# Low parts of forty expert tiles made early, kept in DRAM and loaded again

## The reference

```
qb = (xb @ w_q).reshape(TOKEN_BLOCK, PEER_HEADS, 2, PEER_DKEY)
s = jnp.einsum('thcd,hcnd->thcn', qb, sub_keys)
s_top, i_top = lax.top_k(s, PEER_TOPK)
...
best, pos = lax.top_k(cand, PEER_TOPK)
eidx = jnp.take_along_axis(cand_idx, pos, axis=-1)
g = jax.nn.softmax(best, axis=-1)
h = jax.nn.gelu(jnp.einsum('td,thkd->thk', xb, u[eidx]), approximate=False)
out = jnp.einsum('thk,thkd->td', g * h, v[eidx])
```

## Time and profile before

| | us |
|---|---|
| median of 3 runs | 1611.57 (1611.14 to 1612.08) |
| profiled execution | 1614.49 |
| its span in the profile | 1612.7 |
| TensorE busy (PE) | 1577.1 (98%) |
| VectorE busy (DVE) | 1281.4 (79%) |
| ScalarE busy (ACT) | 630.0 (39%) |
| GpSimd busy (POOL) | 517.4 (32%) |
| data moved | 427.05 MB |

### The profile page before, as it was taken

How to read it: one execution, slowest core, us unless ns; L and a number is a source line. 1 busy time by engine, 2 the same in 40 slices (tenths; PEclk the granted TensorE clock), 3 DMA queues, 4 the chain that set the end, 5 groups by cost and what they waited for, 6 DMA issues and landing times.

```text
span 1612.7 us, 24488 instructions
## 1 busy us (share of the span) xinstructions
PE 1577.1 (98%) x9566; PEld 1389.2 (86%) x9566; DVE 1281.4 (79%) x2390; ACT 630.0 (39%) x996; POOL 517.4 (32%) x261
## 2 busy tenths in 40 slices
PE   9999999999999999899999989999999999999998
PEld 7897977888989999889999988888888888888886
DVE  3024366246899999999998789999999999999997
ACT  5324445523223333345455333333333434333332
POOL 4433232361235778421010233333332232222200
PEclk9999999999999999999999999999999999999999
DMA  5342112133124669699998999999999999999972
GB/s 203 142 149 84 58 53 79 60 135 147 53 92 138 186 199 303 214 331 315 350 354 256 291 420 398 392 396 394 387 391 422 413 409 415 392 391 410 399 297 78
DMA packets 141633, 427.05 MB, mean 265 GB/s; under 512 B 11344, under 2 KB 73040, under 8 KB 120272
## 3 DMA queue, kind: packets, MB, share of 16 engines
q1 hardware_dynamic: 118224, 274.47, 46.9%
q0 software_dynamic: 23296, 151.04, 23.8%
HBM read 378.77 MB, written 46.14 MB: 263 GB/s over the span
## 4 chain that ended last, share of the span: by engine, by line
PE 62%; DVE 31%; DMA 3%; issue 2%; ACT 1%; POOL 0%; SPq 0%; DVEq 0%
PE bank L1437 19%; PE bank L1439 18%; PE bank L1438 18%; DVE wlo L1265 5%; DVE acc L1311 4%; DVE uvb L1273 4%; PE bank L1743 3%; DMA raw<-in_u 2%; DVE idx L1179 1%; DVE idx L1171 1%; DVE val L1170 1%; DVE val L1178 1%; DVE tmp L1172 1%; DMA raw<-in_uv 1%; DVE uvb L1283 1%
## 5 line engine op out<-in xcount | busy, mean ns | idle before, releaser
L1437 PE MATMUL bank<-xhi,whi 128*128 128x352 f32 (+1 forms) x1408 | 491.2, 349 | 22.8 <-DVE wlo L1265 13.8
L1439 PE MATMUL bank<-xhi,wlo 128*128 128x352 f32 (+1 forms) x1408 | 480.8, 341 | 0.0
L1438 PE MATMUL bank<-xlo,whi 128*128 128x352 f32 (+1 forms) x1408 | 480.7, 341 | 0.0
L714 POOL DMA_INDIRECT uvb<-in_uv,eidx x128 | 200.2, 1564 | 571.9 <-DVE acc L1311 422.3
L896 ACT ACTIVATE whi<-raw 128x1024 fp32r<-128x1024 f32 x255 | 268.7, 1055 | 207.1 <-PE bank L1439 148.8
L1437 PEld LDWEIGHTS bank<-xhi,whi 128*128 128x128 f32 x1408 | 265.2, 188 | 50.6 <-DVE wlo L1265 25.1
L1265 DVE TENSOR_TENSOR wlo<-raw,whi 128x1024 fp32r<-128x1024 f32 x215 | 261.9, 1219 | 44.6 <-ACT whi L896 44.4
L1437 PE MATMUL bank<-whi,ahi 128*128 128x512 f32 x762 | 296.7, 389 | 0.0
L1438 PE MATMUL bank<-wlo,ahi 128*128 128x512 f32 x762 | 296.7, 389 | 0.0
L1439 PE MATMUL bank<-whi,alo 128*128 128x512 f32 x762 | 296.5, 389 | 0.0
L1439 PEld LDWEIGHTS bank<-xhi,wlo 128*128 128x128 f32 x1408 | 265.3, 188 | 15.5
(11 more groups left out here) (225 smaller groups left out, 1860.8 us busy)
## 6 DMA issues: line engine op xcount, KB each, us to landing
raw<-in_u SPq DMA_DIRECT2D x128, 512.0 KB, 6.3
raw<-in_uv SPq DMA_DIRECT2D x127, 512.0 KB, 9.2
g_scratch<-stage SPq DMA_DIRECT2D x48, 512.0 KB, 6.9
gl<-g_scratch SPq DMA_DIRECT2D x32, 768.0 KB, 9.6
raw<-in_w_in SPq DMA_DIRECT2D x22, 1024.0 KB, 4.9
h_scratch<-hout SPq DMA_DIRECT2D x96, 192.0 KB, 5.3
hl<-h_scratch SPq DMA_DIRECT2D x24, 768.0 KB, 11.0
raw<-in_w_q SPq DMA_DIRECT2D x6, 1024.0 KB, 4.7
```

What stands on the lines that cost most here:

```text
L714: nc.gpsimd.indirect_dma_start(out=uvb[:, r % UVB, :], out_offset=None, in_=a["uv"][:, :], in_offset=bass.IndirectOffsetOnAxis(ap=eidx[:, ...
L1437: mm(out, lh, rh, start=first, stop=False)
L1438: mm(out, lh, rl, start=False, stop=False)
L1439: return mm(out, ll, rh, start=False, stop=last)
```

## The change

For the first 40 u tiles (`NPRE`) the low part is made during the projections and attention and put into a DRAM tensor. ScalarE issues the loads and stores and makes a rounded copy, VectorE subtracts. 13 turns (`PRE_PROJ` = 40 - 27) stand behind the evacuations of the last projection tiles before attention, one in each of the 27 slots of attention. Three buffers of 4 KB a partition and one for the copy lie in the place of `xn`, so x is loaded there later, once all stores have landed. In the u stage SP loads such a tile's low part beside the tile itself; GpSimd makes none, and has only its gathers. The step constants move some four to six steps forward, and the pairs of sums are spread anew.

```diff
-FIRST_FUSED = 96
+FIRST_FUSED = 92
-POOL_ONLY = 40
-EXP_STEP = 39
-NORM_STEP = 43
-PICKS_TILE = 42
-PICKS_STEP = 46
-HOT0, HOT1, HOT2 = 48, 86, 90
-C_STEPS = [41, 42, 43, 44, 45, 47] + [49 + 3 * i for i in range(NCP - 6)]
-C_TILE, C_STEP = 80, 80
+NPRE = 40
+DVE_FIRST = 34
+EXP_STEP = 34
+NORM_STEP = 37
+PICKS_TILE = 37
+PICKS_STEP = 41
+HOT0, HOT1, HOT2 = 42, 80, 84
+C_STEPS = [34, 35, 36, 38, 39, 40] + [43 + 3 * i for i in range(NCP - 6)]
+C_TILE, C_STEP = 76, 76
-GL_FIRST, GL_SECOND = 95, 99
+GL_FIRST, GL_SECOND = 90, 94
-SUM_STEPS = [89, 91, 93, 95] + [97 + i * 59 // 29 for i in range(29)] + [156 + i * 94 // 31 for i in range(31)]
+SUM_STEPS = [84, 86, 88, 90] + [92 + i * 68 // 29 for i in range(29)] + [160 + i * 90 // 31 for i in range(31)]
...
+        pre_raw = place("pre_raw", [P, 3, D], F32, xn_at)
+        pre_hi = place("pre_hi", [P, D], F32R, xn_at + 3 * 4 * D)
...
@@ wait_low
-            if s < POOL_ONLY:
-                engine.wait_ge(low_pool, s + 1)
+            if s < NPRE:
+                engine.wait_ge(lo_in[s % 4], 16 * (s // 4 + 1))
...
@@ SP
-            sp.wait_ge(x_split_lo, KD)
-            sp.dma_start(xn[:, :, :], a["x_n"]).then_inc(x_in, 16)
...
+            for i in range(3):
+                sp.wait_ge(pre_out[i], 16 * len(range(i, NPRE, 3)))
+            sp.dma_start(xn[:, :, :], a["x_n"]).then_inc(x_in, 16)
             for g in range(G_WO, G_WQ):
...
@@ SP, tile_load
+                elif s >= NPRE + 4:
+                    wait_low(sp, s - 4)
                 elif s >= 4:
-                    wait_low(sp, s - 4)
+                    sp.wait_ge(tile_hi, s - 3)
...
+                if s < NPRE:
+                    if s >= 4:
+                        sp.wait_ge(h_done, s - 3)
+                    else:
+                        sp.wait_ge(q_done, 14 + 2 * (s // 2))
+                    sp.dma_start(tile_bufs(s)[2].bitcast(F32), lo_dram[s]).then_inc(lo_in[s % 4], 16)
...
@@ GpSimd
-            for s in range(POOL_ONLY):
-                tile_low(s)
...
+            pool.wait_ge(cidx_done, 1)
...
+            for j in range(NCP):
                 gather_u(j)
...
@@ ScalarE
+            def pre_load(i):
+                if i >= 3:
+                    act.wait_ge(pre_out[i % 3], 16 * (i // 3))
+                act.dma_start(pre_raw[:, i % 3, :], a["u"][i]).then_inc(pre_in[i % 3], 16)
+
+            def pre_store(i):
+                act.wait_ge(pre_low, i + 1)
+                act.dma_start(lo_dram[i], pre_raw[:, i % 3, :]).then_inc(pre_out[i % 3], 16)
+
+            def pre_turn(i):
+                if i >= 1:
+                    pre_store(i - 1)
+                if i + 1 < NPRE:
+                    pre_load(i + 1)
+                act.wait_ge(pre_in[i % 3], 16 * (i // 3 + 1))
+                nc.scalar.activation(pre_hi[:, :], pre_raw[:, i % 3, :], ACT.Copy).then_inc(pre_high, 1)
...
             for n in range(2 * N_DIL):
                 proj_evac(n)
+                if n == 3:
+                    act.wait_ge(x_split_lo, KD)
+                    pre_load(0)
+                if n >= 2 * N_DIL - PRE_PROJ:
+                    pre_turn(n - 2 * N_DIL + PRE_PROJ)
...
@@ ScalarE, slot s of attention, after the exponentials and before the squares
+                pre_turn(PRE_PROJ + s)
...
@@ VectorE
+            def low_ahead(i):
+                dve.wait_ge(pre_high, i + 1)
+                r = pre_raw[:, i % 3, :]
+                V.tensor_tensor(r, r, pre_hi[:, :].bitcast(F32), ALU.subtract).then_inc(pre_low, 1)
+
+            for i in range(PRE_PROJ):
+                low_ahead(i)
...
@@ VectorE, at the end of slot s of attention
+                low_ahead(PRE_PROJ + s)
...
-            for s in range(POOL_ONLY, 2 * NT):
-                tile_low(s)
+            for s in range(DVE_FIRST, 2 * NT):
+                if s >= NPRE:
+                    tile_low(s)
```

More of the change, by code:

```diff
@@ L208, in program @@
         xlo = keep("xlo", [P, KD, S], F32R)
+        xn_at = at["top"]
         xn = keep("xn", [P, TC, D])
+        pre_raw = place("pre_raw", [P, 3, D], F32, xn_at)
+        pre_hi = place("pre_hi", [P, D], F32R, xn_at + 3 * 4 * D)
         raw = keep("raw", [P, 2, GC])
@@ L387, in program @@
         g_dram = nc.dram_tensor("g_scratch", [NT // 4, P, SETS, 4, SET], F32, kind="Internal").ap()
+        lo_dram = nc.dram_tensor("lo_scratch", [NPRE, P, D], F32, kind="Internal").ap()
         def sem(name):
@@ L422, in program @@
         traw = [sem(f"traw{i}") for i in range(4)]
-        tile_hi, low_pool, low_dve = sem("tile_hi"), sem("low_pool"), sem("low_dve")
+        tile_hi, low_dve = sem("tile_hi"), sem("low_dve")
+        pre_in = [sem(f"pre_in{i}") for i in range(3)]
+        pre_out = [sem(f"pre_out{i}") for i in range(3)]
+        pre_high, pre_low = sem("pre_high"), sem("pre_low")
+        lo_in = [sem(f"lo_in{i}") for i in range(4)]
         h_done, h_gelu = sem("h_done"), sem("h_gelu")
@@ L438, in wait_low @@
         def wait_low(engine, s):
-            if s < POOL_ONLY:
-                engine.wait_ge(low_pool, s + 1)
+            if s < NPRE:
+                engine.wait_ge(lo_in[s % 4], 16 * (s // 4 + 1))
             else:
-                engine.wait_ge(low_dve, s + 1 - POOL_ONLY)
+                engine.wait_ge(low_dve, s + 1 - NPRE)
         def wait_group(engine, g):
@@ L464, in program @@
         SLOTS = UNITS + 3
+        PRE_PROJ = NPRE - SLOTS
         FRONT, HEAD_START = (0, 15, 28), 5
@@ L687, in _ @@
                            allow_small_or_imprecise_dtypes=True).then_inc(iota_done, 1)
[L689 to L693, removed]
             def ring_free(r):
@@ L716, in gather @@
                     in_offset=bass.IndirectOffsetOnAxis(ap=eidx[:, k:k + 1], axis=0)).then_inc(uv_in[r % UVB], 16)
-            for s in range(POOL_ONLY):
-                tile_low(s)
-                if s == GATHER_TILE:
-                    pool.wait_ge(cidx_done, 1)
-                    for g in range(CG):
-                        nc.gpsimd.dma_start(cidx4[g * CT:(g + 1) * CT, :], cidx[CP:P, g * CT:(g + 1) * CT]).then_inc(cidx_in, 16)
-                if s == GATHER_TILE + 1:
-                    pool.wait_ge(cidx_in, 16 * CG)
-                if GATHER_TILE < s <= GATHER_TILE + UVB:
-                    gather_u(s - GATHER_TILE - 1)
-            for j in range(UVB, NCP):
+            pool.wait_ge(cidx_done, 1)
+            for g in range(CG):
+                nc.gpsimd.dma_start(cidx4[g * CT:(g + 1) * CT, :], cidx[CP:P, g * CT:(g + 1) * CT]).then_inc(cidx_in, 16)
+            pool.wait_ge(cidx_in, 16 * CG)
+            for j in range(NCP):
                 gather_u(j)
@@ L838, in _ @@
                 proj_evac(n)
+            pre_store(NPRE - 1)
             act.wait_ge(norm_a, 1)
```

1 line of the change is left out of this document (removed).

## The result

The changed kernel takes 1633.9 us (median of 4 runs, 1632.4 to 1636.8) against 1611.7 us for the kernel before in the same comparison: a ratio of 1.0137, 95% interval 1.0125 to 1.0150. It is 22 us slower; forecast were 12 us. The profiled execution took 1632.5 us, 18.0 us more than that of before (its span is 1630.7 us, also 18.0 more).

The account below looks back on a forecast made before the run. TensorE was taken to set the end, so only its waits could be given back. Profiled 1614.5 - 10.2 (selection) - 8 (mixed stage) + 30 (attention loop) = 1626.3 us, by the median 1623.4 us; range 1600 to 1636 us.

Parts of the forecast that it names:

- the loop of the differential slots: Attention's 16 differential slots: copy and subtraction lengthen each slot's chain, 30 us after slack; 17 with free issues, 38 at most.
- the signs named: If right: one-hots 20 us earlier, no tile 40 wait, logit waits in slots 11 to 26; wrong: waits for lo loads.
- 3.1 us for a turn: Each of forty turns: two ScalarE issues 0.8 us, copy 1.05, subtraction 1.18, with signals, all in series in a differential slot.
- Rival (b): ScalarE's issues nearly free, loop costs 17 us: 1610.4 us, no change; chance 0.15.
- The dilated slots: Eight turns in attention's dilated slots, covered because TensorE takes about twice as long there: cost 0, bound 3 us.
- The selection: Selection without GpSimd's forty low parts: five stretched VectorE lines lose 20.2 us, so selections end by 642.6 us.
- the 10.2 forecast: Gain around the selection: 4.2 us wait at tile 40, 1.5 for GpSimd, 3.1 for one-hots, 1.45 of clock.
- The u stage: Low-part loads for 40 u tiles raise the DMA share from 0.58 to 0.92 before gathers: cost 0, bound 8 us.
- rival (d): U stage starves as lows, tiles and gathers share full engines: 8 us more than the 30 us loop case, 1631 us; chance 0.07.
- The mixed stage: Alternating u and v tiles: sums spread over 68 steps take back 8 of 9.6 us of low-part waits, bounds 0 and 9.6.
- Rival (c): Turn hidden in attention's slots, 1593 us, or partly covered (loop at most 13 us), 1606 us; chance together 0.23.
- Rival (e): Short TensorE holes in attention lower its clock: up to 46 us more, 1669 us; chance 0.03.

Follow-up runs that it names:

- late_low: Changed kernel with VectorE's subtraction of each turn moved into the next slot, behind its reduce and beside the exponentials: 1625.3 us, ratio to before 1.0063.
- dma_only: Changed kernel without copy and subtraction of the 19 turns in the differential slots, loads and stores kept: 1616.8 us (one run; before 1613.7).
- before_68: Kernel before with only the sums respaced: 29 pairs in 68 steps, then 31 in 86: 1607.6 us, ratio 0.9953.
- sums59: Changed kernel with the first 29 pairs of sums in 59 steps instead of 68, the other 31 in 99: 1638.6 us, ratio to before 1.0148.
- before_even: Kernel before with the first 29 pairs of sums one step earlier, on u steps instead of v steps: 1613.6 us against 1614.7, ratio 0.9995.
- small_lo: Changed kernel loading only 128 of 1024 columns of each low part from tile 4 on: 1627.4 us (one run; before 1614.3).

## Why the prediction came out as it did

**The sign and the mechanism held.** Attention was to lose about 30 us in the loop of the differential slots, by copy and subtraction in series with the exponentials. The rows show that order, the lag was 22.6 us there, and undoing one half (late_low) or all (dma_only) of the computing gives 11.1 and 17.8 us back by the last transpose of y.

Of the signs named: first u tile 29.05 us later (forecast 30), TensorE's waits for logits up to 2.1 us but 9 and not 16, the first one-hot matmuls 17.3 us earlier counted from the first u tile (706.1 - 533.1 against 694.4 - 504.1), no wait at tile 40, issues of 0.33 and 0.44 us. The one-hots are a weak sign, since their first step was moved from 48 to 42. And the sign that was to warn of the u stage, TensorE waiting for lo loads, stayed away although the stage failed: TensorE waited for the gelu output instead, and that for the store and the tile loads.

**The loop's price was put together from a wrong part.** Of the 3.1 us for a turn, 0.8 were the issues, which lie under the exponentials: by the rows the turn is 2.3 us, and the sum's own lower bound of 17 us (free issues) would have been the computing alone, for which dma_only gives 18.0. The other 4.6 us stay without the computing and had no term: nothing in the sum let a load land late (4.7 us median, up to 10.9). Rival (b) had the issues right and its total wrong.

**The dilated slots were costed at nothing** because TensorE takes twice as long over them. They cost 5.2 us; waits of 1.5 us for logits and 1.8 us for an evacuation stand at their beginning, the clock was 0.94 between 112 and 140 us. The cover was there in the mean and not in the first slots. With the 1.3 us of the projections this is 6.5 against 0 (bounds 3 each).

**The selection: right in kind, VectorE's lead too small.** The five held lines of the earlier trace rows fell to their minimum (1.226 us for both products). But six more operations were held too, which the prediction's 20.2 us left out. One of them, before and after, count, busy us and mean ns:

```profile
L1205 DVE CAST idf<-idx 128x256 bf16<-128x256 uint32 x4 | 4.5, 1133 | 0.1
```

```profile
L1248 DVE CAST idf<-idx 128x256 bf16<-128x256 uint32 x4 | 1.2, 291 | 0.1
```

The whole selection, from the start of its first cast to the end of its last operation, took 133.0 us before (529.9 to 662.9) and takes 98.5 us after (559.0 to 657.4): 34.5 us less. TensorE gained little of that. It did not wait for a low part at tile 40, but it still waits 2.0 us for one-hots, where the sum took back all 3.1, and tiles 39 to 92 gave 6.6 us, or 5.6 without the moved transposes, where 8.7 of the 10.2 forecast belong. Part of it was luck: another run of the same code as before has 1.2 us of the 4.2 at tile 40 (before_68).

**The u stage was the step that failed.** I gave the DMA engines at a share of 0.92 a cost of 0, bound 8, and rival (d) 0.07. They cost 13.5 us. The mean was right (0.92 between 540 and 590 us); that ten gathers move up into this stretch was in the working and had no number. Up to the burst nothing was lost, in its three tiles 8.3 us, and in the nineteen tiles behind them 5.2. Paced gathers give back 3.9 us, fewer bytes 5.9, the order of issue nothing. Both together were not tried.

**The mixed stage gave 18.0 us, not 8,** more than the bound of its waits, 9.6. The step that failed was to take the idle rows as the loss. A wait of 0.35 us in the trace is 0.62 us of pace: the next matmul would have started 0.23 us behind the last, it starts 0.74 behind, and takes 0.27 instead of 0.16 until the next. 28 pairs of tiles at 8.57 instead of 7.95 us are 17.4 us, nearly the whole 18.0, and that could be read from the distance of two equal rows before. What part of it is spacing (6.2 us by sums59, 11.5 by before_68), what parity (nothing by before_even, though its pairs were faster), what the four tiles fewer and what the lead with which VectorE enters, the runs don't separate.

**Errors of both signs met.** Against the sum the loop was 7.4 too dear, the mixed stage 10.0 too poor, while u tiles 0 to 39, the dilated slots and the small stretches missed 13.5, 5.2 and 1.3 us, and tiles 39 to 92 another 3.6: -7.4 - 10.0 + 13.5 + 5.2 + 1.3 + 3.6 = +6.2 us, the difference of 1632.5 and 1626.3. That the total came so near the truth was luck: it stood on a u stage and a mixed stage that were each missed by 10 us or more.

Rival (c), a hidden turn, fell: the turn adds 1.4 us a slot over its slack. Rival (e) happened in small: the granted clock was 0.96 from 205 to 340 us in place of the 1.00 of the earlier trace rows, at most 5 (0.04 x 135) of the 22.6 us.

## What to carry to other kernels

Work that is moved into an engine's idle time lands at a place in its queue: ask what stands behind it there, not how idle the engine is. Where a stage repeats a rhythm, measure the distance between two equal instructions and hold it against the unhindered distance; idle rows understate the loss. And a stage is not safe because its mean DMA share is below one: the burst of ten gathers cost 8.3 us on a share of 0.92, and still 4.6 us on one of 0.61 (small_lo). Put a burst's bytes at its time.

## What the hardware showed that I had not expected

DMA issues of ScalarE run beside activations already begun; they take 0.33 us (store) and mostly 0.44 us (load), a load at times up to 1.46 us, and the third in a row 0.74 us in the median. Gathers and tile loads together moved 398 GB/s at a share of 1.03, and in that stretch the interval between two gelus rose from 3.84 to 6.8 us. VectorE's early subtractions, two SBUF operands each, were held too: minimum 1.22 us, longest 4.79 us beside a weight's low part on GpSimd. So were VectorE's casts with a single input: 1.13 us on average beside GpSimd's low parts, 0.29 us without them (128x256).
